# Mixer B's scores in a hybrid decoder block: one float32 product per head, or three products of first parts and rests

## The reference

```python
h = rms_norm(x, pre_norm_w[l])
proj = h @ w_in[l]
qa, za, ga, kc, vc, ksl, vsl, kw, vw, qb, kb, vb, zb = jnp.split(proj, splits, axis=-1)
...
oa = nsa_mixer(...)                                   # mixer A, 16 heads, 4 key/value heads
ob = dilated_mixer(to_heads(qb, 16), to_heads(kb, 16), to_heads(vb, 16), positions)   # mixer B
mix = jnp.concatenate([oa * silu(za), ob * silu(zb)], axis=-1)
x = x + rms_norm(mix @ w_out[l], post_norm_w[l])
```

## Time and profile before

| | |
|---|---|
| median of 3 runs | 1837.71 us (1837.62 to 1839.41) |
| the profiled execution | 1837.62 us, its span 1835.8 us |
| TensorE busy | 1824.1 us, 99% of the span, 8474 products |
| TensorE weight loads | 1512.7 us, 82% |
| VectorE busy | 1062.3 us, 58% |
| ScalarE busy | 823.3 us, 45% |
| GpSimd busy | 188.8 us, 10% |
| granted TensorE clock | 1.00 of 2.4 GHz |
| HBM traffic | 187 GB/s over the span |

### The profile page before, as it was taken

The page is one execution under the profiler, slowest core; times in us unless marked ns, Lnnn a source line. Parts: engine busy times, 40 slices in busy tenths (PEclk is TensorE's granted clock), DMA queues, the critical chain, the costliest instruction groups (busy, mean ns, idle before and its releaser), DMA issues.

```text
span 1835.8 us, 23379 instructions
## 1 busy us (share of the span) xinstructions
PE 1824.1 (99%) x8474; PEld 1512.7 (82%) x8474; DVE 1062.3 (58%) x1097; ACT 823.3 (45%) x1062; POOL 188.8 (10%) x161
## 2 busy tenths in 40 slices
PE   9999999999999999999999999999999999999998
PEld 7888878888888888888888888888888888888886
DVE  7856656556665665644564456445644584445444
ACT  6644454444544435444444444444444464444442
POOL 2220002200202020022002200220022000000000
PEclk9999999999999999999999999999999999999999
DMA  9866677546455464666566656665666667776665
GB/s 290 249 194 186 190 230 222 167 124 189 129 168 164 128 182 127 183 186 193 162 193 186 193 162 192 187 191 163 188 190 190 177 184 218 211 210 204 214 206 193
DMA packets 183928, 344.78 MB, mean 188 GB/s; under 512 B 15136, under 2 KB 19360, under 8 KB 183840
## 3 DMA queue, kind: packets, MB, share of 16 engines
q1 hardware_dynamic: 182992, 342.45, 64.1%
q10 hardware_dynamic: 848, 1.07, 0.2%
HBM read 339.27 MB, written 4.19 MB: 187 GB/s over the span
## 4 chain that ended last, share of the span: by engine, by line
PE 98%; DVE 1%; DMA 0%; ACT 0%; issue 0%; DVEq 0%; ACTq 0%
PE acc L445 30%; PE acc L447 30%; PE acc L446 30%; PE trans L459 2%; PE heads L488 2%; PE scores L473 2%; PE acc L606 1%; PE heads L527 0%; DVE y L1291 0%; PE scores L595 0%; PE scores L506 0%; DMA xt_raw<-in_x_t 0%; PE trans L516 0%; ACT w_parts L717 0%; PE trans L649 0%
## 5 line engine op out<-in xcount | busy, mean ns | idle before, releaser
L947 DVE TENSOR_TENSOR w_parts<-raw,w_parts 128x1024 fp32r<-128x1024 f32 x624 | 779.9, 1251 | 695.6 <-ACT w_parts L717 695.2
L717 ACT ACTIVATE w_parts<-raw 128x1024 fp32r<-128x1024 f32 x624 | 660.3, 1059 | 735.3 <-PE acc L447 728.3
L445 PE MATMUL acc<-w_parts,x_parts 128*128 128x512 f32 x2432 | 961.1, 395 | 3.7 <-DVE w_parts L947 1.7
L447 PE MATMUL acc<-w_parts,x_parts 128*128 128x512 f32 x2432 | 948.2, 390 | 0.0
L446 PE MATMUL acc<-w_parts,x_parts 128*128 128x512 f32 x2432 | 947.0, 389 | 0.0
L447 PEld LDWEIGHTS acc<-w_parts,x_parts 128*128 128x128 f32 x2432 | 456.5, 188 | 97.4
L445 PEld LDWEIGHTS acc<-w_parts,x_parts 128*128 128x128 f32 x2432 | 456.9, 188 | 96.2 <-issue 5.0
L446 PEld LDWEIGHTS acc<-w_parts,x_parts 128*128 128x128 f32 x2432 | 457.1, 188 | 91.3
L400 POOL TENSOR_TENSOR rot<-tok_a,trig 128x512 f32<-128x512 f32 x26 | 41.1, 1579 | 1127.6 <-ACT tok_a L723 936.3
L729 ACT ACTIVATE probs_t<-trans 128x512 f32<-128x512 f32 (+1 forms) x44 | 26.2, 596 | 88.0 <-PE trans L459 81.0
L1199 DVE RECIPROCAL mixed<-mixed 128x256 f32<-128x256 f32 x32 | 55.9, 1747 | 0.5
(11 more groups left out here) (151 smaller groups left out, 581.2 us busy)
## 6 DMA issues: line engine op xcount, KB each, us to landing
raw<-in_w_in SPq DMA_DIRECT2D x480, 512.0 KB, 3.6
raw<-in_w_out SPq DMA_DIRECT2D x128, 512.0 KB, 4.5
raw<-in_w SPq DMA_DIRECT2D x16, 512.0 KB, 4.5
x_tok<-in_x SPq DMA_DIRECT2D x16, 256.0 KB, 4.9
xt_raw<-in_x_t SPq DMA_DIRECT2D x7, 512.0 KB, 5.9
out<-y SPq DMA_DIRECT2D x5, 512.0 KB, 2.9
wpost<-in_post_w SPq DMA_DIRECT2D x8, 256.0 KB, 4.9
gate_raw<-in_w_in SPq DMA_DIRECT2D x1, 768.0 KB, 8.0
```

The costliest lines, as they stand in the source:

```text
L445: nc.tensor.matmul(o, stat_hi, w_hi[:, s, kk, 0:width], start=(k == 0), stop=False)
L447: last = nc.tensor.matmul(o, stat_lo, w_hi[:, s, kk, 0:width], start=False, stop=(k == KB - 1))
L717: nc.scalar.activation(w_hi[:, n % SPLIT_SLOTS, :, 0:width], raw[:, n % RAW_SLOTS, :, 0:width], ACT.Copy).then_inc(hi_ready, 1)
L947: V.tensor_tensor(w_lo[:, s, :, 0:width], raw[:, n % RAW_SLOTS, :, 0:width], w_hi[:, s, :, 0:width].bitcast(F32), ALU.subtract).then_inc(l ...
```

## The change

Mixer B's queries and keys are kept as first parts and rests as well, and its scores are three fp32r products per head and tile instead of one float32 product.

- `first_parts` takes the place of `take_fill` on ScalarE for the q and k fills of mixer B: it copies the fill, rounded to fp32r, to `qb_hi` or `kb_hi`, and counts in the new semaphore `bhi_ready` instead of releasing the bank.
- `rest_parts` is new on VectorE: it waits for the fill and for the first part, writes fill minus first part to `qb_lo` or `kb_lo`, and releases the bank. In VectorE's stream it stands just behind the `split` of pair at + 3, for at = 4 and 5.
- `split_scores` takes the place of `unit_scores` in `attention_b`: first by first, first by rest, rest by first. Waits and units are the same.
- The four new buffers lie on memory that is no longer used: `qb_hi` on `qrot_t`, `qb_lo` on `v_tok[:, 1]`, `kb_hi` and `kb_lo` on the two halves of `k_t`.

```diff
+            def split_scores(u, unit, fills):
+
+                t, h0, nh = UNITS[u]
+                pe.wait_ge(tr_free, fills)
+                pe.wait_ge(scores_free, unit)
+                nk = P * (t + 1)
+                for h in range(h0, h0 + nh):
+                    o = scores[:, (h - h0) * nk:(h - h0 + 1) * nk]
+                    q = [part[:, h, t * P:(t + 1) * P] for part in (qb_hi, qb_lo)]
+                    keys = [part[:, h, 0:nk] for part in (kb_hi, kb_lo)]
+                    nc.tensor.matmul(o, q[0], keys[0], start=True, stop=False)
+                    nc.tensor.matmul(o, q[0], keys[1], start=False, stop=False)
+                    last = nc.tensor.matmul(o, q[1], keys[0], start=False, stop=True)
+                last.then_inc(scores_done, 1)
...
-                    unit_scores(u, unit + u, qrot_t, lambda h, nk: k_t[:, 0, h, 0:nk], fill)
+                    split_scores(u, unit + u, fill)
...
+            def first_parts(fill, dst, ready):
+
+                act.wait_ge(tr_done, fill + 1)
+                nc.scalar.activation(dst, trans[:, :].rearrange("p (h t) -> p h t", h=HPG), ACT.Copy).then_inc(ready, 1)
...
-                            dst = qrot_t if j == 0 else k_t[:, 0, :, :]
-                            take_fill(FILL_B + 2 + 2 * j + t + FILLS_B * g, dst[:, :, t * P:(t + 1) * P])
+                            dst = qb_hi if j == 0 else kb_hi
+                            first_parts(FILL_B + 2 + 2 * j + t + FILLS_B * g, dst[:, :, t * P:(t + 1) * P], bhi_ready)
                         split(C_B + 1 + j + 4 * g, n)
...
+            def rest_parts(fill, dst, hi, ready, count):
+
+                dve.wait_ge(tr_done, fill + 1)
+                dve.wait_ge(ready, count)
+                V.tensor_tensor(dst, trans[:, :].rearrange("p (h t) -> p h t", h=HPG), hi.bitcast(F32), ALU.subtract
                                 ).then_inc(tr_free, 1)
...
                         split(C_B + 1 + j + 4 * g, n)
+                        if n - LEAD in (4, 5):
+                            t = n - LEAD - 4
+                            cols = slice(t * P, (t + 1) * P)
+                            lo, hi = ((qb_lo, qb_hi), (kb_lo, kb_hi))[j]
+                            rest_parts(FILL_B + 2 + 2 * j + t + FILLS_B * g, lo[:, :, cols], hi[:, :, cols], bhi_ready,
+                                       4 * g + 2 * j + t + 1)
```

More of the change, by code:

```diff
@@ L124, in build @@
         k_t, late = sb("k_t", [P, 2, HPG, SEQ])
-        v_tok, _ = sb("v_tok", [P, 2, TILES, NC])
+        v_tok, v_off = sb("v_tok", [P, 2, TILES, NC])
         qraw_t, q_off = sb("qraw_t", [P, HPG, SEQ])
-        qrot_t, _ = sb("qrot_t", [P, HPG, SEQ])
+        qrot_t, r_off = sb("qrot_t", [P, HPG, SEQ])
         probs, p_off = sb("probs", [P, 4, NC])
+        qb_hi, _ = sb("qb_hi", [P, HPG, SEQ], F32R, offset=r_off)
+        qb_lo, _ = sb("qb_lo", [P, HPG, SEQ], F32R, offset=v_off + 4 * TILES * NC)
+        kb_hi, _ = sb("kb_hi", [P, HPG, SEQ], F32R, offset=late)
+        kb_lo, _ = sb("kb_lo", [P, HPG, SEQ], F32R, offset=late + 4 * HPG * SEQ)
         x_tok, _ = sb("x_tok", [P, TILES, D_MODEL], offset=late)
@@ L222, in build @@
         tr_free = sem("tr_free")
+        bhi_ready = sem("bhi_ready")
         scores_done = sem("scores_done")
@@ L957, in take_fill @@
                 V.tensor_scalar(dst, trans[:, :].rearrange("p (h t) -> p h t", h=HPG), 1.0, None, ALU.mult
+                                ).then_inc(tr_free, 1)
+            def rest_parts(fill, dst, hi, ready, count):
+                dve.wait_ge(tr_done, fill + 1)
+                dve.wait_ge(ready, count)
+                V.tensor_tensor(dst, trans[:, :].rearrange("p (h t) -> p h t", h=HPG), hi.bitcast(F32), ALU.subtract
                                 ).then_inc(tr_free, 1)
```

## The result

The changed kernel takes 1846.53 us (median of 6 runs, 1846.15 to 1847.38) against 1837.87 for the kernel before (6 runs): ratio 1.0046, 95% interval 1.0036 to 1.0056, 8.7 us slower. 1846.8 was forecast.

The account below looks back on a forecast made before the run. TensorE's own instruction stream, busy 99%, was taken to bound the kernel. 1837.6 us + 9.0 for eight stalls + 0.2 for the products = 1846.8 us, range 1843 to 1853.

Parts of the forecast that it names:

- The wait that moves: Second transposes after Q and K in mixer B: bank released by VectorE's subtraction behind a split, 0.85 us late, eight times.
- case: The forecast's main case: eight TensorE stalls of about 1.1 us in mixer B, score products even; 60%.
- The price of a stall: TensorE at a late bank release: lateness 0.85 us plus restart 0.25 to 0.34; 1.12 taken, eight times 9.0 us.
- The products: Mixer B's scores: 24 fp32r products a group take 2.66 us against 2.61, +0.2 us over four groups.
- Rival 1: Mixer B's scores: narrow fp32r products cost 0.227 us like wide ones; 1852.5 us (22%), or 1858.0 with 256 columns too (5%).
- Rival 2: Mixer B's scores: the weight load sets no floor for fp32r, products -2.3 us instead of +0.2; 1844.3 us, 7%.
- rival 3: Mixer B's fills: VectorE subtracts before TensorE wants the bank, so only products count; 1837.8 us, 4%.

Follow-up runs that it names:

- e1: Changed kernel with VectorE's subtraction put ahead of the split of pair at + 3, not behind it: 1838.79 us, ratio 1.0006 to the kernel before.
- e4: Changed kernel with the transposes of tile 1, their copy and subtraction moved from pair 5 to pair 6: 1838.56 us, ratio 1.0005.
- e2: Changed kernel with the float32 score products of the kernel before, first parts unrounded, rests written but not used: 1846.06 us, ratio 1.0045.
- e3: Changed kernel with each subtraction done twice, first into a scratch tile: 1851.24 us, ratio 1.0073.
- e5: Kernel of e1 with each score product multiplying only half of its keys (64 columns for tile 0, 128 for tile 1): 1837.84 us, one run.
- e6: Kernel of e1 with each score product loading only the first 64 of its tile's 128 queries as weights: 1835.59 us, one run.
- e7: Kernel before with three fp32r products only for tile 1, float32 kept for tile 0, parts made by VectorE from SBUF: 1836.14 us, ratio 0.9992.

## Why the prediction was right

Time, direction and mechanism came out as forecast: 8.7 us against 9.2. Step by step:

- *The wait that moves.* Right, and with it the choice of case. The queue was read correctly: the subtraction starts 0.08 before the split's end, and the release is 0.83 us late where 0.85 was forecast. Shown by e1 and e4, which remove it in two ways, by e2, which keeps it alone, and by e3, which makes it longer.
- *The price of a stall.* This is the one term with an error to speak of: 1.12 forecast, 0.99 measured, 1.0 us of the sum. The part on top of the lateness was read at the output projection as 0.25 to 0.34; it is 0.14 to 0.16 here (842.80 against a release at 842.66, and 0.02 behind). Why the restart is cheaper in front of transposes wasn't tried. The measured 0.99 lies below the 1.10 to 1.19 that the prediction worked out, about half way between the 1.12 and its low bound, the lateness alone.
- *The products.* +0.05 a group forecast, +0.15 measured. The narrow ones were 0.108 in the forecast and are 0.111; the wide ones were 0.113, by columns, and are 0.119. Rival 1 (a narrow product as dear as a wide one, or a form that falls back) is refuted by the trace after, 1.35 us for the 12 where it needs 2.7. Rival 2 (no floor) is refuted by the same rows, as it needs 0.68, and by e5, and e6 shows that the floor is the load.
- *The hidden wait* (rival 3) did not occur in the change. Its mechanism, however, is exactly e1, and its forecast, 1837.8, is close to the 1838.8 measured there.
- *Luck.* The two errors, -1.0 us and +0.4, offset each other in part. And the time came nearer (1846.53 for 1846.8) than the change (8.7 for 9.2), since the kernel before measured 1837.87 here and not the 1837.6 that the sum starts from.

## What to carry to other kernels

When the release of a buffer moves to another engine, follow that engine's queue to the place of the new instruction and ask what it has to wait for in turn: here a subtraction of 0.69 us, for which the engine had time, cost TensorE 0.99 us at each of eight places, and moving one line gave it back. A small fp32r product cost TensorE about the larger of two prices, that of its columns and that of its load of weights: splitting a float32 product in three gained at 256 columns of moving data (0.36 against 0.43 us) and lost at 128 (0.33 against 0.22); the gain is seen in the trace of e7, while its times can't yet be told from the kernel before. And where a wait exists only because two things stand one pair apart, moving either of them is as good.

## What the runs showed of the hardware

An fp32r product of 128 columns of weights and 64 or 128 of moving data takes 0.111 us of the stream, one of 256 takes 0.119, one of 512 0.227; with 64 columns of weights it takes 0.059 for 128 of moving data and 0.115 for 256. I had not expected the wide one to stay over half of the 512-column price (0.113), and no run says why it does. Two PSUM subtractions in a row on VectorE are 0.60 us apart though each is recorded as 0.68.
